# Attention order of a two-path decoder step: two steps of the item ahead between two scores of the next

## The chip, the cores and the metric

One core of a Trainium2 chip runs the whole program. The metric is the device time of one execution in microseconds, the median of three runs. PE is the matrix engine, DVE the vector engine, ACT the scalar engine, POOL the general engine, SP the queue that issues most DMAs.

## The reference, cut to what matters

The program is one inference step of a small decoder: a convolution layer, then keys and values from a single projection, then one layer of sparse attention, each followed by a gated feed-forward network, for a prompt of 512 rows and eight sample sequences of 8 rows. The changed part is the attention layer. It adds three softmax branches, each weighted by a sigmoid gate:

```
s_c = q . kc * scale - slope * d_c ; o_c = softmax(s_c, d_c >= 0) . vc      # compressed keys
s_s = q . ks * scale - slope * d_s ; o_s = softmax(s_s, d_s >= 0) . vs      # selected blocks
s_w = q . kw * scale - slope * d_w ; o_w = softmax(s_w, window) . vw        # sliding window
o = g[0] * o_c + g[1] * o_s + g[2] * o_w                                    # then o @ w_o
```

With 512 rows every block is selected, so the prompt computes two dense causal branches and a compressed one of 31 keys.

## The kernel before, in words

The prompt's attention is cut into 16 items, one for each of 4 key heads and 4 blocks of 128 query rows. `PROMPTS` gives their order as (key head, row block i); an item with row block i has rows of L = 128(i+1) keys. Items 0 to 15 have i = 1, 3, 3, 1, 1, 2, 3, 0, 3, 0, 2, 0, 2, 1, 2, 0. Each item goes through these steps:

- `score` n.a, four times (L2173 on PE): q times keys for two heads of one branch into a pair of PSUM banks. DVE adds the slope term, writes the row to `Pp` and takes its minimum (L1615); ACT takes the exponential and the row's sum (L1075). There are two bank pairs, so a score on PE waits until DVE is through with the last but one.
- `cmp` n (L2184 on PE): the same for the compressed branch into `Pc`; DVE L1625 to L1632, then ACT L1116.
- `weigh` n: DVE turns sums into weights (L1641 to L1652), the last of these scaling `Pc`; POOL multiplies the eight rows of `Pp` by them (L676), the four of the first branch first.
- `turn` n.x (L1776 on PE): the transposes of one block of 128 keys for four heads. Block 0 is the compressed one and waits for the weights (L1652); block 1 is the first of the first branch and waits for POOL's first four multiplications. An item has 2(i+1)+1 blocks: 3, 5, 7 or 9. A copy to one of four buffers `PT` (DVE L1696 or ACT L1088, in turns) empties the bank; there are two such banks. A copy also waits until the product that read this `PT` buffer last is done.
- `prod` n.x (L2220 on PE): block times values, added up in PSUM.
- `out`: ACT rounds the sum to `Oh` (L1132), DVE writes the rest to `Ol` (L1741).

The samples have steps of their own: `s_keys`, `s_score`, `s_weigh`, `s_turn`, `s_prod` (L2290), `s_oturn`, with `SMP_FRONT` and `SMP_BACK` naming the group in which they stand.

`_attention_plan` writes all of these into one list, `ATT`. Each engine's program walks that list and emits its own part of each step, so the list is the order of PE, DVE, ACT and POOL alike, and an instruction that waits holds up all that stands behind it on its engine. A group j of the list holds the scores and `cmp` of item j (`new`), the turns and products of item j-1 (`old`, from `_back`), and the samples' steps. The first part of a group, `seq`, alternates scores with old steps; what is left of `old` is mixed with the samples' steps in `rest`, and `weigh` j is put in at place 4 of `rest`, or at its end if `rest` is shorter.

After the list comes the output projection with `w_o`. Its first weights go to the same memory as buffers of the samples (`PTs`), so SP loads them only after the last `s_prod`.

Of the kernel before, what the change touches and what calls it, by code (L numbers as in the profile page):

```python
# [136 lines left out]
def _blocks(n):  # L137

    i = KVI(n)[1]
    return [(2, 0)] + [(br, kb) for br in range(2) for kb in range(i + 1)]  # L140


def _back(n):

    steps = len(_blocks(n))
    out = []
    for x_ in range(0, steps, 2):
        out += [("turn", n, y) for y in range(x_, min(x_ + 2, steps))]
        if x_:
            out += [("prod", n, x_ - 2), ("prod", n, x_ - 1)]  # L150
    return out + [("prod", n, steps - 1)]


def _attention_plan():

    plan, items = [], []

    def put(m):
        plan.append(m)
        if m[0] == "s_prod" or m[0] == "prod" and m[2] == len(_blocks(m[1])) - 1:  # L160
            items.append(("sample" if m[0] == "s_prod" else "prompt", m[1]))
            plan.append(("out", len(items) - 1, 0))

    for j in range(len(PROMPTS) + 1):
        more = j < len(PROMPTS)
        new = [("score", j, a) for a in range(4)] + [("cmp", j, 0)] if more else []
        old = _back(j - 1) if j else [("s_gates", 0, 0), ("p_gates", 0, 0)] + [("vc", h, 0) for h in range(4)]
        seq = new[:1]
        for k in range(1, len(new)):
            seq += old[:1] + new[k:k + 1]  # L170
            old = old[1:]
        smp = []
        for b in range(NB):
            if SMP_BACK[b] == j:
                smp += [("s_turn", b, 0), ("s_turn", b, 1), ("s_prod", b, 0), ("s_oturn", b, 0)]
        for b in range(NB):
            if SMP_FRONT[b] == j:
                smp += [("s_keys", b, 0), ("s_keys", b, 1), ("s_score", b, 0), ("s_weigh", b, 0)]
        rest, n_old, n_smp = [], 0, 0
        while n_old < len(old) or n_smp < len(smp):  # L180
            if n_smp < len(smp) and (n_smp * max(len(old), 1) < n_old * len(smp) or n_old == len(old)):
                rest.append(smp[n_smp])
                n_smp += 1
            else:
                rest.append(old[n_old])
                n_old += 1
        if more:
            rest.insert(4, ("weigh", j, 0))
        for m in seq + rest:
            put(m)  # L190
    return plan, items


ATT, ITEMS = _attention_plan()
SLOT = {m: k for k, m in enumerate(m for m in ATT if m[0] in ("score", "cmp", "s_score"))}
TURN = {m: k for k, m in enumerate(m for m in ATT if m[0] in
# [2238 lines left out]
```

## Time and profile before

| | |
|---|---|
| median of 3 runs | 1767.98 us (1763.5 to 1768.83) |
| profiled execution: its own time, its span | 1751.85 us, 1750.1 us |
| busy share of the span | PE 93%, DVE 49%, ACT 36%, POOL 9% |
| mean granted clock of PE | 0.973 |
| attention, from the first score to the last product | 989 to 1235 us of the span |

The page gives busy time over the whole span. Outside the attention PE is busy nearly without a break; within it all four engines take turns, and the stretch has to be read for itself. Times in the rows below are microseconds from the start of the span, unless a column is marked otherwise.

### The profile page before, as it was taken

How to read it: one execution, taken by the hardware profiler on the slowest of the kernel's cores; microseconds unless marked ns; L12 is line 12 of the kernel's file. 1: busy time of each engine (PE TensorE's matmuls, PEld its weight loads, DVE VectorE, ACT ScalarE, POOL GpSimd, SP SyncE). 2: the span in 40 equal slices, each digit the busy share in tenths (PEclk: the TensorE clock that was granted, in tenths of full speed). 3: DMA queues.
4: the chain of work that ended last, by engine and by line, in shares of the span. 5: the costliest groups of instructions: out<-in, count | busy, mean ns of one | idle time of the engine just before them, and what ended most of it. 6: DMA issues, size and time to landing. Idle time of an engine off the chain costs nothing.

```text
span 1750.1 us, 33973 instructions
## 1 busy us (share of the span) xinstructions
PE 1620.8 (93%) x14265; PEld 1480.4 (85%) x14265; DVE 857.3 (49%) x1646; ACT 631.7 (36%) x1263; POOL 164.5 (9%) x284
## 2 busy tenths in 40 slices
PE   5899868999999999999999999889899999999996
PEld 4788747899999999999899755445789999999995
DVE  5899955563232223355344377666474233223234
ACT  4455566342221222232214556545243221122223
POOL 2000001300000000001100255333000000000000
PEclk8999989999999999998999999988999999999998
DMA  9999853633332333322313510110322232222311
GB/s 325 294 320 325 296 176 118 186 96 113 101 106 73 97 97 108 98 61 79 95 50 90 147 28 2 49 38 12 103 67 85 85 107 75 73 78 81 112 34 55
DMA packets 236401, 198.34 MB, mean 113 GB/s; under 512 B 7058, under 2 KB 195810, under 8 KB 235984
## 3 DMA queue, kind: packets, MB, share of 16 engines
q1 hardware_dynamic: 229600, 172.25, 32.4%
q0 software_dynamic: 6352, 23.88, 4.7%
q8 instruction: 113, 1.85, 0.4%
q14 instruction: 32, 0.26, 0.0%
q10 hardware_dynamic: 304, 0.10, 0.0%
HBM read 188.87 MB, written 11.20 MB: 114 GB/s over the span
## 4 chain that ended last, share of the span: by engine, by line
PE 78%; DVE 7%; DMA 7%; ACT 4%; issue 3%; POOL 1%; POOLq 0%; SPq 0%; DVEq 0%; ACTq 0%
PE ps L1796 58%; DMA ada<-in_w_ada_dram 4%; PE ps L1776 4%; PE ps L1847 4%; PE ps L1812 2%; PE ps L2173 2%; PE ps L2220 2%; PE ps L2098 1%; DMA xrows<-in_x_sample_dram 1%; PE ps L1834 1%; PE ps L2290 1%; DVE t L1230 1%; DMA C<-in_cache_kv_dram 1%; DVE wl L1164 1%; PE ps L2074 1%
## 5 line engine op out<-in xcount | busy, mean ns | idle before, releaser
L714 ACT ACTIVATE wh<-raw 128x1024 fp32r<-128x1024 f32 (+1 forms) x173 | 193.1, 1117 | 706.5 <-PE ps L1796 686.4
L1796 PE MATMUL ps<-Hh,wh 128*128 128x288 f32 x1952 | 425.1, 300 | 7.8 <-DVE Hl L1395 3.7
L1796 PE MATMUL ps<-Hh,wl 128*128 128x288 f32 x1952 | 420.4, 297 | 0.0
L1796 PE MATMUL ps<-Hl,wh 128*128 128x288 f32 x1952 | 420.3, 297 | 0.0
L1164 DVE TENSOR_TENSOR wl<-raw,wh 128x1024 fp32r<-128x1024 f32 (+1 forms) x173 | 223.7, 1293 | 225.3 <-ACT wh L714 224.4
L1796 PEld LDWEIGHTS ps<-Hh,wh 128*128 128x128 f32 x1952 | 317.2, 191 | 10.3 <-issue 7.4
L1796 PEld LDWEIGHTS ps<-Hh,wl 128*128 128x128 f32 x1952 | 316.2, 190 | 0.2
L1796 PEld LDWEIGHTS ps<-Hl,wh 128*128 128x128 f32 x1952 | 316.0, 189 | 0.2
L1796 PE MATMUL ps<-al,wh 128*128 128x288 f32 x616 | 132.0, 296 | 0.0
L1796 PE MATMUL ps<-ah,wh 128*128 128x288 f32 x616 | 131.9, 296 | 0.0
L1796 PE MATMUL ps<-ah,wl 128*128 128x288 f32 x616 | 131.9, 296 | 0.0
L1518 DVE TENSOR_TENSOR t<-ps,t 128x576 f32<-128x576 f32 x44 | 33.4, 758 | 169.0 <-PE ps L1796 167.3
L1320 DVE TENSOR_TENSOR rtmp<-ps,mods 128x64 f32<-128x64 f32 x40 | 9.0, 224 | 196.4 <-PE ps L1796 176.1
L1812 PE MATMUL ps<-ada,cpad 128*32 128x128 f32 x2048 | 71.3, 287 | 31.5 <-DMA ada<-in_w_ada_dram 27.1
L676 POOL TENSOR_TENSOR Pp<-Pp,wgt 128x256 f32<-128x256 f32 (+3 forms) x128 | 88.3, 722 | 118.3 <-DVE wgt L1646 118.3
L1796 PEld LDWEIGHTS ps<-ah,wl 128*128 128x128 f32 x616 | 99.3, 189 | 0.0
L1796 PEld LDWEIGHTS ps<-ah,wh 128*128 128x128 f32 x616 | 99.3, 189 | 0.0
L1796 PEld LDWEIGHTS ps<-al,wh 128*128 128x128 f32 x616 | 99.3, 189 | 0.0
L1812 PEld LDWEIGHTS ps<-ada,cpad 128*32 128x32 f32 x2048 | 56.8, 115 | 42.0 <-DMA ada<-in_w_ada_dram 32.4
L1075 ACT ACTIVATE Pp<-Pp,nmin 128x256 f32<-128x256 f32 (+3 forms) x128 | 70.3, 550 | 26.4 <-DVE nmin L1615 26.1
L1459 DVE SCALAR_TENSOR_TENSOR y<-u_p,wdT,y 128x512 f32<-128x512 f32 x98 | 73.1, 746 | 0.0
L1459 DVE SCALAR_TENSOR_TENSOR r<-u_p,wdT,r 128x512 f32<-128x512 f32 x98 | 73.1, 746 | 0.0
(336 smaller groups left out, 2261.8 us busy)
## 6 DMA issues: line engine op xcount, KB each, us to landing
ada<-in_w_ada_dram SPq DMA_DIRECT2D x64, 1024.0 KB, 8.3
raw<-in_ffn_w_up_dram SPq DMA_DIRECT2D x88, 512.0 KB, 3.8
raw<-in_ffn_w_down_dram SPq DMA_DIRECT2D x32, 704.0 KB, 4.6
raw<-in_conv_w_pw_dram SPq DMA_DIRECT2D x24, 512.0 KB, 9.0
raw<-in_w_kv_dram SPq DMA_DIRECT2D x12, 512.0 KB, 3.8
C<-in_cache_kv_dram POOLq DMA_DIRECT2D x32, 128.0 KB, 3.6
out_win_sample_dram<-in_state_win_dram POOLq DMA_DIRECT2D x8, 512.0 KB, 3.7
raw<-in_nsa_w_in_dram SPq DMA_DIRECT2D x8, 512.0 KB, 3.9
```

What stands on the lines that cost most here:

```text
L676: nc.gpsimd.tensor_tensor(Pp[:, n % 2, s, 0:L], Pp[:, n % 2, s, 0:L], wgt[:, n % 2, s:s + 1].to_broadcast([P, L]), ALU.mult).then_inc(S("s ...
L714: A(wh[:, u % RING, 0:K, 0:w], raw[:, u % RING, 0:K, 0:w], ACT.Copy).then_inc(hi_ready, 1)
L1075: A(Pp[:, n % 2, s, 0:L], Pp[:, n % 2, s, 0:L], ACT.Exp, scale=-1.0, bias=nmin[:, n % 2, s:s + 1], accum_out=sums[:, n % 2, s:s + 1]).then ...
L1164: V.tensor_tensor(wl[:, u % RING, 0:K, 0:w], raw[:, u % RING, 0:K, 0:w], wh[:, u % RING, 0:K, 0:w].bitcast(F32), ALU.subtract).then_inc(lo ...
L1459: V.scalar_tensor_tensor(acc[k % 2], u_p[:, j, bass.ds(i * per + k, TP)], wdT[:, bass.ds(i * (per * DC) + (k * DC + j), 1)], acc[k % 2], A ...
L1518: V.tensor_tensor(t, tile(u0 + 2 * p + 1), t, ALU.mult).then_inc(tile_free, 2)
L1776: return nc.tensor.transpose(out, in_, ident[0:in_.shape[0], 0:in_.shape[0]])
L1796: last = M(ps[0:w, 2 * s + h, 0:HT], wt[:, s, k, 0:w], rt[:, k, h * HT:(h + 1) * HT], start=(k == 0 and i == 0), stop=(k == K - 1 and i == 2))
L1812: last = M(strip_bank(s_)[32 * g:32 * g + 32], cpad[:, 4 * hf + k, :], ada[:, n % RING_ADA, k, g * P:g * P + P], start=(hf == 0 and k == 0 ...
L1847: last = M(ps[:, 2 * s + h, 0:HT], wt[:, s, k, :], rt[:, k, h * HT:(h + 1) * HT], start=(k == 0 and i == 0), stop=(k == K - 1 and i == 2))
L2173: last = M(ps[:, 2 * (k % 2) + par, 0:L], qT[rows_, 2 * kv + a // 2, P * i:P * i + P], keys[rows_, 2 * br + kv // 2, 0:L], start=True, sto ...
L2220: last = M(ps[64 * par:64 * par + 64, 6 + it % 2, 0:2 * P], v, PT[TURN[("turn", n, x_)] % 4][0:K].rearrange("p (g q) -> p g q", g=G)[:, pa ...
```

## The change

Between two scores of the next item stand two steps of the item ahead, where there was one. Nothing else is edited; the steps, their number and their instructions are the same.

```
         seq = new[:1]
         for k in range(1, len(new)):
-            seq += old[:1] + new[k:k + 1]
-            old = old[1:]
+            seq += old[:2] + new[k:k + 1]
+            old = old[2:]
```

`seq` takes eight old steps in place of four, so `rest` is shorter by four. An item of five blocks has ten old steps, one of three blocks has six; for these `rest` may be shorter than four, and `weigh` goes to its end, behind `out`.

On PE, at the end of group 4 and the start of group 5 (both old items have five blocks). Before, from the compressed scores of item 4: five products and one turn of item 3, then a score of item 5 (L2173, 384 wide), the turn of item 4's block 0 (`Pc`), and a second score; behind it stands the turn of block 1 (`Pp`).

```order
L2184 MATMUL ps<-kcT_p_68,qT_65 128x31 x4
L2220 MATMUL ps<-PT2_99,vc_p_69 64x256 x2
L2220 MATMUL ps<-PT3_100,vrow_81 64x256 x2
L1776 MATMUL ps<-ident_124,Pp_101 128x128 x4
L2220 MATMUL ps<-PT0_97,vrow_81 64x256 x2
L2220 MATMUL ps<-PT1_98,vrow_81 64x256 x2
L2220 MATMUL ps<-PT2_99,vrow_81 64x256 x2
L2173 MATMUL ps<-kvT_64,qT_65 128x384
L2173 MATMUL ps<-Ksw_82,qT_65 128x384
L1776 MATMUL ps<-ident_124,Pc_102 31x128 x4
L2173 MATMUL ps<-kvT_64,qT_65 128x384
L2173 MATMUL ps<-Ksw_82,qT_65 128x384
```

The same place on PE in the changed kernel:

```order
L2184 MATMUL ps<-kcT_p_68,qT_65 128x31 x4
L2220 MATMUL ps<-PT1_98,vrow_81 64x256 x2
L2220 MATMUL ps<-PT2_99,vrow_81 64x256 x2
L2173 MATMUL ps<-kvT_64,qT_65 128x384
L2173 MATMUL ps<-Ksw_82,qT_65 128x384
L1776 MATMUL ps<-ident_124,Pc_102 31x128 x4
L1776 MATMUL ps<-ident_124,Pp_101 128x128 x4
```

Between `cmp` and the turn of block 1 stood five products, a turn, two scores and the turn of block 0; now two products, one score and the turn of block 0 stand there.

On DVE at the same place, before: the compressed scores, a copy, the weights of item 4, and then `Ol` of item 3.

```order
L1632 TENSOR_TENSOR Pc_102<-Pc_102,slk_144 128x124
L1696 COPY PT2_99<-ps 128x512
L1641 TENSOR_REDUCE sums_92<-Pc_102 128x4
L1643 RECIPROCAL wgt_93<-sums_92 128x12
L1646 TENSOR_TENSOR wgt_93<-wgt_93,gates_89 128x8
L1647 TENSOR_TENSOR wgt_93<-wgt_93,gates_89 128x4
L1652 TENSOR_TENSOR Pc_102<-Pc_102,wgt_93 128x124
L1741 TENSOR_TENSOR Ol_67<-ps,Oh_66 128x2x128
```

And in the changed kernel:

```order
L1632 TENSOR_TENSOR Pc_102<-Pc_102,slk_144 128x124
L1741 TENSOR_TENSOR Ol_67<-ps,Oh_66 128x2x128
L1641 TENSOR_REDUCE sums_92<-Pc_102 128x4
L1643 RECIPROCAL wgt_93<-sums_92 128x12
L1646 TENSOR_TENSOR wgt_93<-wgt_93,gates_89 128x8
L1647 TENSOR_TENSOR wgt_93<-wgt_93,gates_89 128x4
L1652 TENSOR_TENSOR Pc_102<-Pc_102,wgt_93 128x124
```

`Ol` moved ahead of the weights, and the copy is no longer between.

On DVE in group 8 (old item of three blocks) of the changed kernel, the last two scores of item 8 with `Ol` of item 7 between them; before, the copy of a turn stood there and `Ol` came behind the weights of item 8.

```order
L1615 ISA Pp_101,nmin_91<-ps,dist_115 128x512
L1615 ISA nmin_91 128x1
L1741 TENSOR_TENSOR Ol_67<-ps,Oh_66 128x2x128
L1615 ISA Pp_101,nmin_91<-ps,dist_115 128x512
L1615 ISA nmin_91 128x1
L1615 ISA Pp_101,nmin_91<-ps,dist_115 128x512
L1615 ISA nmin_91 128x1
L1625 TENSOR_TENSOR Pc_102<-ps,distc_137 128x2x31 x2
```

All three products of item 7 and its `out` are now done within the scores of item 8.

## Rows read from the trace of the kernel before

**Rows 1.** Windows: busy us (instructions) of each engine, granted clock, DMA share, GB/s.
```profile
988.00:1240.00 252.00, 220.55 (x2125) 126.75 (x2124) 173.04 (x607) 137.99 (x431) 100.52 (x146) 0.95 0.18 49
...
1150.60:1160.80 10.20, 9.77 (x46) 6.51 (x47) 6.22 (x31) 5.27 (x20) 2.22 (x6) 0.50 0.01 2
1177.90:1191.50 13.60, 11.52 (x124) 6.89 (x124) 4.21 (x17) 3.14 (x12) 5.82 (x9) 0.50 0.30 79
```

**Rows 2.** Waits within 988 to 1240: us in total, times, longest.
```profile
PEld ps L1776 <- ACT PT L1088: 7.9, 13, 1.0
```

**Rows 3.** Pieces of the chain that ended last: start, us, what.
```profile
995.46 0.59 PE ps L2184 x8
...
1001.86 1.06 PE ps L2173 x4
...
1008.92 4.08 POOL Pp L676 x4
...
1041.48 1.46 PE ps L2290 x56
1042.93 1.01 PE ps L2220 x8
...
1058.66 0.59 PE ps L1776 x4
1059.25 0.87 PE ps L2173 x4
...
1064.28 3.23 POOL Pp L676 x4
```

**Rows 4.** Timeline from `cmp` of item 4 to its turn of block 1; idle before in brackets.
```profile
1050.90 0.63 PE L2184 MATMUL ps<-kcT_p,qT 64*128 64x31 f32 x8
...
1051.58 0.35 DVE L1625 TENSOR_TENSOR Pc<-ps,distc 128x62 f32<-128x62 f32 x2 [0.34 <-PE ps L2184]
...
1052.99 0.31 ACT L1116 ACTIVATE Pc<-Pc 128x124 f32<-128x124 f32 x1 [0.35 <-DVE Pc L1632]
...
1053.92 0.27 DVE L1641 TENSOR_REDUCE sums<-Pc 128x4 f32<-128x124 f32 x1
...
1054.74 3.51 POOL L676 TENSOR_TENSOR Pp<-Pp,wgt 128x256 f32<-128x256 f32 x6 [11.90 <-DVE wgt L1646]
...
1054.77 0.38 ACT L1132 ACTIVATE Oh<-ps 128x256 fp32r<-128x256 f32 x1 [1.48 <-PE ps L2220]
...
1055.42 0.41 DVE L1741 TENSOR_TENSOR Ol<-ps,Oh 128x256 fp32r<-128x256 f32 x1
...
1057.16 0.66 PE L1776 MATMUL ps<-ident,Pp 128*128 128x128 f32 x4
```

**Rows 5.** Timeline of PE: turn of block 1 of item 1; score of item 11.
```profile
1013.05 0.66 PE L1776 MATMUL ps<-ident,Pp 128*128 128x128 f32 x4 [1.21 <-POOL Pp L676]
...
1151.03 0.58 PE L2173 MATMUL ps<-kvT,qT 64*128 64x128 f32 x1 [2.01 <-DVE nmin L1615]
```

**Rows 6.** Timeline of group 8: an exponential, `cmp`, and the first `s_prod`.
```profile
1104.72 0.71 ACT L1075 ACTIVATE Pp<-Pp,nmin 128x512 f32<-128x512 f32 x1
1104.83 0.64 PE L2184 MATMUL ps<-kcT_p,qT 64*128 64x31 f32 x8
...
1108.16 0.43 PE L2290 MATMUL ps<-Cs,PTs 128*32 128x64 f32 x16 [1.20 <-ACT PTs L1104]
```

**Rows 7.** Timeline of group 7, behind `s_score` of sample 2.
```profile
1094.55 0.69 DVE L1696 COPY PT<-ps 128x512 f32<-128x512 f32 x1 [3.19 <-PE ps L2220]
...
1095.16 0.48 DVE L1664 CUSTOM_DVE_ANT_0 Ps<-ps,tabs 128x320 f32<-128x320 f32 x1
...
1097.70 0.65 PE L2220 MATMUL ps<-PT,vrow 128*64 128x256 f32 x4 [1.24 <-ACT PT L1088]
```

**Rows 8.** Chain and timeline at the end of the attention.
```profile
1229.94 5.75 DMA raw<-in_nsa_w_o_dram
...
1239.86 0.82 PE L1796 MATMUL ps<-Oh,wh 128*128 128x288 f32 x2 [4.45 <-DVE wl L1164]
```

## Prediction

> **What bounds the kernel now.** The page puts most of the span on PE, so I read the attention alone, by windows. In its 252 us PE is busy for 220.55 [rows 1], which leaves 31.5 us of idle time: the whole of what a new order could win, as the order changes no instruction. The idle time is spread over many short waits. The view of waits shows who is waited for: PE's transposes wait 7.9 us, in 13 waits, for ACT's copies [rows 2], the largest share that has one cause. POOL waits for the weights, 11.90 us before item 4 [rows 4]: it has little to do, but it does it late, right before PE needs it. The chain of work then gives the price of each step on PE from its start to the next one's: a score is 1.06 us at 512 keys and 0.87 at 384, a turn 0.59, two products 1.01, `cmp` 0.59, `s_prod` 1.46 [rows 3]; for a score of 128 keys I estimate 0.42 from these. Last I read the timeline at every place where one item hands over to the next.
>
> The scores themselves hardly wait: score, turn, score, turn run at 1.06 + 0.59 and 0.87 + 0.59 in the chain, with PE as its only member. More cover between two scores is therefore worth nothing there. What counts is where the cover is taken from.
>
> **The hand-over of five-block items.** The chain from `cmp` of item n to its turn of block 1 is read from item 4 [rows 4]. `cmp` starts at 1050.90; DVE begins 0.68 later, and ACT's exponential starts at 1052.99 and lasts 0.31, so it ends 2.40 after `cmp`'s start. The weights start 0.82 before POOL does (1053.92 to 1054.74). POOL's first half ends and the turn starts 2.42 later (1057.16). With nothing in between this is 2.40 + 0.82 + 2.42 = 5.6 us for 256 keys. PE has to have that much work between the two steps, or it idles.
>
> Before, item 4 has five products (2.6), two turns (1.2), two scores (1.7) and `cmp` (0.6) there, 6.1 us for a distance of 6.26: an idle time of 0.2. After, it has `cmp`, two products, one score and one turn: 0.59 + 1.01 + 0.87 + 0.59 = 3.06 us. The chain has also grown, as `Ol` now stands ahead of the weights on DVE and needs `Oh`, which stands behind the exponential on ACT: 0.38 + 0.41 [rows 4] and two handovers, 0.85. So the turn of block 1 starts 6.5 us after `cmp`, PE idles 3.4, and the loss is 3.2.
>
> The same sum for the three others of this kind. Item 5 has 384 keys: POOL 3.23 [rows 3] in place of 2.42, distance 7.3, work 0.59 + 1.01 + 1.06 + 0.59 = 3.25, idle 4.05, against 0.35 before by the same count: 3.7. Item 1 has 512 keys: POOL 4.08 [rows 3], distance 8.2, idle 4.95, against 1.21 [rows 5] and 0.2 at the turn before it: 3.5. Item 0: no `out` is ahead, distance 5.6, work 0.59 + 1.06 + 0.59 = 2.24, idle 3.4 against 0.6: 2.8. **Together 13.2.** The bounds are 9 (the queue of DVE is emptier and the weights come 1 us earlier in each case, against my reading) and 16 (it is fuller: before, item 1 took 0.7 more than the bare chain).
>
> **Items behind three-block items (8, 10, 12).** Their group has `cmp`, then the samples' turns and `s_prod`, whose input is copied by DVE and ACT behind the compressed scores. Before, `s_prod` started 3.33 us after `cmp` with 1.20 of idle time [rows 6]. Two things change. The two products 7.0 and 7.1, 1.1 us, that stood around `cmp` are now ahead of the last score. And `Ol` stands between the last two scores on DVE: it waits for ACT to take the second exponential of the score before (0.71, [rows 6]), then 0.38 for `Oh` and 0.41 for itself, 1.5 us in which the last score isn't processed. Item 8 loses 2.6. For 384 keys I take 2.2 each. **Together 7.0**, bounds 1.8 (only one product's cover, 0.6 each) and 8.
>
> **Item 14.** Its `weigh` now has behind it only `s_prod`, a score of 128 keys and a turn, and ahead of it `Ol` of item 13. From `cmp`, work is 0.59 + 1.01 + two sample turns 0.95 + 1.46 + 0.15 + 0.42 + 0.59 = 5.2; the chain is 2.4, about 1.0 for copies of the sample's turns on DVE, 0.85 for `Oh` and `Ol`, 0.4 of handovers, 3.23 for POOL, 7.9. Idle 2.8 against 0.75 before: **2.1** (bounds 1 and 3). Items 2, 3, 6 to 13 have a sample's steps or many old steps behind `weigh` (6.8 us or more of work from `cmp`), so I cost them at nothing; item 6 is at the edge, with 1.0 of new idle time in exchange for as much that it had a few steps later.
>
> **The end.** The weights of `w_o` are fetched once the last `s_prod` is through: the DMA starts at 1229.94, takes 5.75, and PE idles 4.45 until 1239.86 [rows 8]. The change puts a turn and a product of item 14, that stood behind the last `s_prod`, ahead of it: 0.59 + 0.5, **1.1**, with nothing to hide it.
>
> **What is gained.** In groups 2, 7 and 9 a copy on DVE waits 3.19 us for a product that PE has behind `s_score` [rows 7], since both use one `PT` buffer. It holds up DVE's part of `s_score`, which starts at 1095.16, and the last product, which idles 1.24. In the new order that product stands ahead of `s_score`. DVE can then start when `s_score` ends, 1.25 earlier, but the two products no longer fill PE either: idle about 1.0, gain 0.3, three times. The waits for such copies at turns 5 and 6 and at `s_keys` in groups 2, 3, 7 and 9 come to about 4 of the 7.9 us [rows 2], of which I take 2.6 as gone. In groups 6, 11 and 13 the last product waited 0.4 to 0.5 and two turns 0.2 to 0.3 for the same reason: 2.0. **Together 5.5 less**, bounds 0 and 10; the upper one is the 7.9 us and the rest of the three gaps.
>
> **The clock.** In two stretches of the attention, 10.2 and 13.6 us long, the granted clock is 0.50, which is 1.2 GHz, in place of 1.00; the first began while PE idled for 2.01 us [rows 5]. PE is busy for 9.77 and 11.52 us in them [rows 1]. At full clock that work takes at least half of it, so one costs at most 4.9 and 5.8. The new order makes some seven gaps of 2.3 to 3.8 us. I take **6.0** more, a little over one such stretch, between minus 8 (both present ones gone) and plus 30.
>
> The Trainium skill (TensorE: Matmul & The Clock Gate, HAM oscillation) says that gaps in PE's work make the gate halve its rate, so that the work behind each gap starts slow. By that rule, applied to every gap, the clock would cost about 34 and not 6. This trace agrees only in part: the clock fell at the gap of 2.01 us, and at those of 1.20 to 1.24 it did not [rows 5 to 7].
>
> **The sum.** 13.2 + 7.0 + 2.1 + 1.1 - 5.5 + 6.0 = 23.9 us on an execution of 1751.85 (span 1750.1 and 1.75 around it): 1775.8, or 1.37% more. The three runs have their median at 1767.98, 0.9% above the profiled execution, so the forecast is 1767.98 x 1.0137 = 1792.
>
> **The rivals.** (A) *The clock falls at every new gap.* Seven times 4.9 is 34 in place of 6: 1751.85 + 17.9 + 34 = 1804, by the median 1820. For it speaks that the gaps are longer than the one ahead of 1150; against it, that several of them are broken by a turn, and pieces of 1.2 us kept the full clock [rows 5 to 7]. (B) *Faster: the copies stop blocking, and POOL's half is covered.* If the weights come as early against PE's work as they do now, only the gain remains, 5.5 to 10, and the time is 1758 to 1762. It decides at the turn of block 1: it wins if the distance from `cmp` is no longer than PE's work of 3.1 to 3.3 us. The bare chain of 5.6 speaks against that, since POOL alone takes 2.4 to 4.1 of it. (C) *No change.* The idle time at the hand-overs lets DVE and ACT catch up and is won back in the next scores. That needs scores that wait for DVE or ACT, and the chain shows PE alone there. 1768. (D) *Half of it:* the three-block items lose only one product's cover and the clock stays as it is: 13.2 + 1.8 + 2.1 + 1.1 - 5.5 = 12.7, by the median 1781, at the lower side of the forecast.
>
> **How the numbers follow.** The forecast's own case, with (D) in it, has 0.76, A 0.13, B 0.05, C 0.06. The range reaches from 1777, a little under (D), to 1806, which takes in a clock loss of 20; it leaves out most of A, and B and C. A measurement of this kernel tells 0.3% from no change, 5 us. Faster 0.05, same 0.05, slower 0.90 (a part of C is a small loss).
>
> **What would show it.** In the trace after: the turn of block 1 of items 0, 1, 4 and 5 waits for POOL with 1 to 3 us of idle time, and the turn of block 0 ahead of it for DVE's L1652 with 2 to 3; `s_prod` in groups 8, 10 and 12 waits about 3.5 us; DVE's L1741 in group 8 waits for ACT; the last product of groups 2, 7 and 9 waits 1.0; `w_o`'s DMA starts as many us later as the attention has lost. PE's busy time in the attention stays at 220, but for the clock. The prediction is wrong if the DVE part of `cmp` starts much earlier or later than 0.7 us behind PE's, or if the clock drops more often.

## Result: 2.6% slower, in the attention alone, and about half of it by the clock

| | before | changed |
|---|---|---|
| median of the runs | 1765.74 us (4 runs, 1760.65 to 1768.83) | 1806.76 us (4 runs, 1799.87 to 1810.04) |
| ratio of the two | | 1.0257, interval 1.0214 to 1.0299 |
| profiled execution, its time and span | 1751.85, 1750.1 us | 1799.87, 1798.1 us |
| mean granted clock of PE | 0.973 | 0.952 |

The forecast was 1792 us, 1.37% more, with a range to 1806; the time lies above it. The direction was right and the size was about half.

The page after: busy time of each engine, and the granted clock in 40 slices, in tenths.

```profile
PE 1645.6 (92%) x14265; PEld 1494.9 (83%) x14265; DVE 860.0 (48%) x1649; ACT 634.0 (35%) x1260; POOL 164.7 (9%) x284
...
PEclk8999989999999999999999898877799999999997
```

The instructions of PE are as many as before, yet PE is busy for 1645.6 us and not 1620.8. The digits of the clock say why: in slices 23 to 29, the attention, they read 8 9 8 8 7 7 7. The windows after, of the attention and of three stretches in it (columns as in [rows 1]):

```profile
985.00:1288.00 303.00, 246.97 (x2126) 143.02 (x2125) 175.83 (x610) 140.05 (x428) 100.59 (x146) 0.83 0.15 41
...
1209.20:1222.80 13.60, 10.64 (x134) 6.77 (x128) 4.89 (x18) 2.37 (x9) 6.36 (x8) 0.50 0.30 79
1134.10:1144.30 10.20, 8.79 (x85) 6.06 (x86) 5.13 (x21) 2.73 (x12) 8.07 (x8) 0.50 0.58 155
1168.20:1178.50 10.30, 8.59 (x114) 6.05 (x115) 3.59 (x14) 2.50 (x9) 6.35 (x8) 0.50 0.33 103
```

Against [rows 1] the attention is 51 us longer (303 for 252). PE is busy 26.4 us longer (246.97 for 220.55) and idle 24.6 us longer (56.0 for 31.45). The mean clock is 0.83 in place of 0.95. With two levels, 1.00 and 0.50, that is about 103 us at 1.2 GHz (303 x 0.17 / 0.5) against 25. So there are two halves to explain: waits, and work at the lower clock. What lies behind the attention is as long as before, and what lies ahead of it 3 us shorter. The profiled execution before took 14 us less than its median and the one after 7 less, so the traces show a loss of 48 us where the medians show 41.

The waits after, in 985 to 1288 (us, times, longest). The first row answers to POOL's wait in [rows 4], the others are PE's own; before, the most that PE's transposes waited for one engine was [rows 2]. A `PEld` row and a `PE` row of the same line are mostly the same waits, seen at the weight load and at the matmul.

```profile
POOL Pp L676 <- DVE wgt L1646: 180.0, 16, 15.8
...
PEld ps L1776 <- DVE Pc L1652: 11.7, 4, 3.3
...
PE ps L1776 <- ACT PT L1088: 9.4, 6, 2.9
...
PE ps L2290 <- ACT PTs L1104: 9.0, 4, 3.2
...
PE ps L1776 <- DVE Pc L1652: 8.6, 4, 2.5
...
PEld ps L1776 <- POOL Pp L676: 8.3, 6, 2.4
```

The first transposes of an item now wait four times for the weights (L1652) and six for POOL, `s_prod` waits for the samples' copies, and transposes wait 9.4 us for ACT's copies on PE, where it was 3.4 before.

**The hand-over of item 4**, timeline after. It answers to [rows 4].

```profile
1060.33 0.64 PE L2184 MATMUL ps<-kcT_p,qT 64*128 64x31 f32 x8
...
1061.01 0.35 DVE L1625 TENSOR_TENSOR Pc<-ps,distc 128x62 f32<-128x62 f32 x2 [0.35 <-PE ps L2184]
...
1062.42 0.31 ACT L1116 ACTIVATE Pc<-Pc 128x124 f32<-128x124 f32 x1 [1.58 <-DVE Pc L1632]
1062.64 0.37 ACT L1132 ACTIVATE Oh<-ps 128x256 fp32r<-128x256 f32 x1
1063.04 0.42 DVE L1741 TENSOR_TENSOR Ol<-ps,Oh 128x256 fp32r<-128x256 f32 x1 [0.65 <-ACT Oh L1132]
1063.38 0.27 DVE L1641 TENSOR_REDUCE sums<-Pc 128x4 f32<-128x124 f32 x1
...
1064.19 3.52 POOL L676 TENSOR_TENSOR Pp<-Pp,wgt 128x256 f32<-128x256 f32 x6 [12.03 <-DVE wgt L1646]
...
1065.00 0.62 PE L1776 MATMUL ps<-ident,Pc 128*31 128x128 f32 x4 [2.18 <-DVE Pc L1652]
...
1066.62 1.12 PE L1776 MATMUL ps<-ident,Pp 128*128 128x128 f32 x4 [0.99 <-POOL Pp L676]
```

From `cmp` to the turn of block 1 it is 6.29 us here and was 6.26 before: the chain of DVE, ACT and POOL has hardly changed, its cover on PE has. PE idles 2.18 and 0.99 us on the way.

**The third turn**, timeline after, of item 11 at the start of group 12. It is a wait that the forecast didn't have.

```profile
1196.14 0.18 DVE L1679 RECIPROCAL wgtS<-sumsS 128x3 f32<-128x3 f32 x1 [1.05 <-ACT Pcs L1126]
...
1196.56 0.79 DVE L1684 TENSOR_SCALAR Pcs<-Pcs,wgtS 128x15 f32<-128x15 f32 x1
...
1197.26 0.41 DVE L1741 TENSOR_TENSOR Ol<-ps,Oh 128x256 fp32r<-128x256 f32 x1
1197.60 0.54 DVE L1615 CUSTOM_DVE_ANT_0 Pp<-ps,dist 128x384 f32<-128x384 f32 x1
...
1199.39 0.57 ACT L1088 ACTIVATE PT<-ps 31x512 f32<-31x512 f32 x1
...
1200.11 0.63 PE L1776 MATMUL ps<-ident,Pp 128*128 128x128 f32 x4 [2.59 <-ACT PT L1088]
```

Read from below: PE waits 2.59 us for ACT to empty the bank of the item's first turn. ACT does that behind the exponentials of the score. The score's part on DVE starts only at 1197.60, though PE gave the score at 1194.77, because DVE stands in the weights of a sample (L1679), which wait for ACT. The same wait is 2.87 us at item 6, 1.95 at 10, 1.91 at 12 and 2.61 at 13; at items 10 and 12 it is for the copy on DVE. There is a second change at this place: between an item's first turn and its third, which needs the same bank, stood two scores and a turn, and now one score and a turn.

**`s_prod` of group 8**, timeline after. It answers to [rows 6].

```profile
1127.89 0.53 PE L2184 MATMUL ps<-kcT_p,qT 64*128 64x31 f32 x8
...
1128.59 0.43 DVE L1741 TENSOR_TENSOR Ol<-ps,Oh 128x256 fp32r<-128x256 f32 x1 [1.25 <-ACT Oh L1132]
...
1131.44 0.41 DVE L1712 COPY PTs<-ps 128x256 f32<-128x256 f32 x1
...
1132.54 0.43 PE L2290 MATMUL ps<-Cs,PTs 128*32 128x64 f32 x16 [3.21 <-ACT PTs L1104]
```

`Ol` waits 1.25 us for `Oh` with the last score behind it, and `s_prod` 3.21 us in place of 1.20.

**The end**, chain and timeline after, which answer to [rows 8]; and the last product of item 6, which answers to the last of [rows 7].

```profile
1278.29 6.68 DMA raw<-in_nsa_w_o_dram
```

```profile
1287.57 0.82 PE L1796 MATMUL ps<-Oh,wh 128*128 128x288 f32 x2 [5.30 <-DVE wl L1164]
...
1119.80 0.44 PE L2220 MATMUL ps<-PT,vrow 128*64 128x256 f32 x2 [1.15 <-ACT PT L1088]
```

### The profile page after: what moved, and what is told of

The parts are those of the page before. It is cut to its first block, busy times and chain, and to the rows that moved or that the text cites. A ratio compares the mean times of both kernels' runs of the same rounds, so it can differ in the third digit from the quotient of the medians.

```text
span 1798.1 us, 33973 instructions
## 1 busy us (share of the span) xinstructions
PE 1645.6 (92%) x14265; PEld 1494.9 (83%) x14265; DVE 860.0 (48%) x1649; ACT 634.0 (35%) x1260; POOL 164.7 (9%) x284
## 3 DMA queue, kind: packets, MB, share of 16 engines
q8 instruction: 113, 1.85, 0.4%
## 4 chain that ended last, share of the span: by engine, by line
PE 78%; DVE 7%; DMA 6%; ACT 4%; issue 3%; POOL 1%; POOLq 0%; SPq 0%; DVEq 0%; ACTq 0%
PE ps L1796 56%; PE ps L1776 5%; PE ps L1847 4%; DMA ada<-in_w_ada_dram 4%; PE ps L1812 2%; PE ps L2220 2%; PE ps L2173 2%; PE ps L2098 1%; DMA xrows<-in_x_sample_dram 1%; POOL Pp L676 1%; PE ps L1834 1%; PE ps L2290 1%; DVE t L1230 1%; DVE wl L1164 1%; DMA C<-in_cache_kv_dram 1%
## 5 line engine op out<-in xcount | busy, mean ns | idle before, releaser
L1776 PEld LDWEIGHTS ps<-ident,Pp 128*128 128x128 f32 x320 | 44.1, 169 | 41.5 <-issue 19.0
L1776 PE MATMUL ps<-ident,Pp 128*128 128x128 f32 x320 | 59.8, 331 | 19.9 <-ACT PT L1088 8.8
```

Source lines behind the costliest of these rows:

```text
L1776: return nc.tensor.transpose(out, in_, ident[0:in_.shape[0], 0:in_.shape[0]])
```

## Experiments

The ratio of each is to the kernel before, run beside it on the same chip.

### The clock: work in the gaps

The changed kernel, with fillers ahead of the steps that wait longest (three of the 17 entries of the table are shown; the bank is that of the next product):

```
+FILL = {('turn', 0, 0): 9, ('turn', 1, 0): 10, ('turn', 1, 1): 8, ...}
...
             for m in ATT:
                 what, n, x_ = m
+                if m in FILL:
+                    it_ = ORD[("prompt" if what == "turn" else "sample", n)]
+                    if it_ >= 2:
+                        pe.wait_ge(S("o_free"), it_ - 1)
+                    for _f in range(FILL[m]):
+                        M(ps[:, 6 + it_ % 2, 0:P], ident[:], ident[:], start=True, stop=True)
```

> The changed kernel with filler matmuls on PE (128x128 of ones and zeros into the PSUM bank of the next product, whose content is overwritten) put ahead of 17 steps that wait 0.8 to 3.2 us in its trace; 3 to 13 of about 0.2 us each, some four fifths of each gap. Theory 1, the clock: over half of the 45 us lost is work at 1.2 GHz behind the gaps (in the profiled run 99 us of the attention at that clock against 24 before, PE busy 27 us longer, PE idle only 24 us longer). With the gaps filled the time at 1.2 GHz falls under 50 us and the whole time by 12 to 25 us against the changed kernel, to 1.3% above before or less. Rival, the waits alone: the hand-overs cost 45 us through DVE, ACT and POOL and the clock is only seen beside them. Then fillers change nothing or add up to 10 us.

Measured: 1778.62 us, ratio 1.0092 (1.0062 to 1.0122). Its windows over the attention, and its timeline at the hand-over of item 4, with the fillers at L2313:

```profile
993.00:1267.00 274.00, 247.31 (x2418) 158.07 (x2416) 176.05 (x610) 139.48 (x428) 100.50 (x146) 0.98 0.17 45
```

```profile
1068.73 2.27 PE L2313 MATMUL ps<-ident 128*128 128x128 f32 x18
1070.98 0.62 PE L1779 MATMUL ps<-ident,Pc 128*31 128x128 f32 x4
1071.44 1.06 PE L2313 MATMUL ps<-ident 128*128 128x128 f32 x8
1072.59 0.66 PE L1779 MATMUL ps<-ident,Pp 128*128 128x128 f32 x4
```

The turns start as late as without fillers, since they wait for the same things: from `cmp` to the turn of block 1 it is 5.98, 8.08, 6.29 and 7.14 us for items 0, 1, 4 and 5 in both traces. But the clock is 0.98 in place of 0.83, and the attention is 29 us shorter. Work that computes nothing takes 1.65 of the 2.57%, some 29 us, a little more than I expected. Theory 1 holds; the rival falls. (The kernel before loses time to the clock too, so these 29 us aren't all a cost of the change; the kernels with fillers below tell how much is.)

The same with transposes as fillers:

```
-                    for _f in range(FILL[m]):
-                        M(ps[:, 6 + it_ % 2, 0:P], ident[:], ident[:], start=True, stop=True)
+                    for _f in range(FILL[m] * 3 // 2):
+                        tr(ps[:, 6 + it_ % 2, 0:P], ident[:])
```

> The changed kernel with the same fillers as the first of these runs, but as transposes in place of matmuls, half as many more of them, as one takes about 0.15 us and not 0.2. With matmuls the time was 0.9% over before and the clock stayed at 2.4 GHz for all but 7 us. If any work on PE holds the clock up, it is the same here, within 5 us. If transposes don't count, the clock falls as in the changed kernel and the time is 2% or more over before.

Measured: 1782.88 us, ratio 1.0126 (1.0073 to 1.0178), and in the attention:

```profile
988.00:1264.00 276.00, 243.98 (x2341) 152.02 (x2341) 175.37 (x610) 139.55 (x428) 100.62 (x146) 0.95 0.17 45
```

A clock of 0.95 against 0.83 without fillers and 0.98 with matmuls, or 24 us at 1.2 GHz against 99 and 7, in one execution each; the two intervals of the time overlap. Transposes hold the clock up here, if perhaps a little less well.

The next two are the kernel before with fillers, first at 11 places, 3 to 8 each, and 18 ahead of the output projection (the same helper, called with the product's number by hand):

```
+FILL = {('s_prod', 1, 0): (8, 4), ('score', 11, 2): (14, 8), ('s_turn', 5, 1): (17, 6), ('prod', 1, 8): (2, 4), ...}
```

> The kernel before with the same fillers, 3 to 8 of them ahead of 11 steps that wait 0.8 to 2.0 us there, and 18 in the gap ahead of the output projection. If the clock costs what the fillers on the changed kernel say (29 us of the attention for 92 us less at 1.2 GHz), the 24 us at that clock here are worth some 7 us: 4 to 8 us faster than before. If fillers only helped because they lay in long gaps, or if they cost as much as they bring, within 3 us of before.

Measured: 1751.13 us, ratio 0.9969 (0.9947 to 0.9991). With fillers at three more places:

> The kernel before with fillers at three more places (before turns 1.5 and 6.2 and s_score of sample 7, 2 to 6 each). The last 10 us at 1.2 GHz in the attention should go too, worth 3 us: 0.3 to 0.6% faster than before. If the fillers now stand in PE's way, it is no faster than the version with 11 places.

Measured: 1751.10 us, ratio 0.9949 (0.9921 to 0.9977). Windows of both over the attention, the one with 11 places first:

```profile
989.00:1239.00 250.00, 231.96 (x2260) 139.93 (x2258) 172.75 (x607) 137.87 (x431) 100.67 (x146) 0.98 0.18 50
```

```profile
989.00:1240.00 251.00, 233.65 (x2283) 142.47 (x2282) 172.78 (x607) 138.09 (x431) 100.68 (x146) 0.99 0.18 49
```

Both are faster than the kernel before, and the second is the fastest version here; whether it beats the first can't be told. By the ratios they bring 5.5 and 9 us, as expected. The attention in the traces is only 1 to 2 us shorter, but the profiled execution before had a mean clock of 0.973, where its runs beside these experiments have 0.955 to 0.974.

These two tell the clock's part in the change. With matmuls as fillers both kernels are at 2.4 GHz in the attention for all but 7 to 10 us, and the changed one is still 1.2 to 1.4% slower (1.0092 against 0.9969 and 0.9949), or 22 to 25 us, of which 1 to 2 us are the fillers ahead of the output projection that it doesn't have. That is the part of the waits; it fits the 24.6 us that PE is idle longer. The other 20 to 25 of the 45 us are the clock.

### Which items carry the loss

Two steps behind items of seven or nine blocks only, and in the other kernel behind those of three or five only:

```
-            seq += old[:2] + new[k:k + 1]
-            old = old[2:]
+            two = 2 if len(_blocks(max(j - 1, 0))) >= 7 and j else 1
+            seq += old[:two] + new[k:k + 1]
+            old = old[two:]
```

> Two steps between scores only where the item ahead has seven or nine blocks; one step, as before, behind items of three or five. By my sum the loss sits at the short items: 13.2 us at four hand-overs, 7.0 behind three-block items, 2.1 at item 14, and two of the new waits at the third turn (items 11 and 13, 5 us) as well, while the long items gain 3 to 5. So PE's idle time returns to that of before or 4 less, the clock falls about as before or for 20 us more, and the time is within 8 us of before on either side. Rival, that two steps are bad for every item (banks of the turns fill up): it keeps at least half of the loss, 20 us or more.

> The complement: two steps only behind items of three or five blocks. If the loss sits at the short items, PE idles 25 us more than before and the clock adds 15 to 25: 35 to 50 us slower than before, all or more of the loss of the whole change. Rival as for the other half: 20 us or less.

Measured: 1772.69 us, ratio 1.0061 (1.0038 to 1.0085), and 1791.83 us, ratio 1.0186 (1.0132 to 1.0240). The windows of the attention of the first and of the second:

```profile
990.00:1259.00 269.00, 230.09 (x2126) 133.17 (x2127) 174.77 (x609) 139.27 (x429) 100.48 (x146) 0.91 0.17 46
```

```profile
987.00:1277.00 290.00, 241.06 (x2129) 140.80 (x2128) 174.25 (x608) 139.55 (x430) 100.66 (x146) 0.86 0.15 43
```

The two parts add up to 2.47%, nearly the whole 2.57%. Three quarters are with the short items, as the forecast had it, though it is a little less than I expected of that half (1.9% for 2.0 to 2.8). But the long ones gain nothing; they lose 0.6%, 11 us, where I had expected 8 at most on either side. The trace of that kernel shows where: the third turns of items 6, 10 and 12 wait 2.87, 3.09 and 1.97 us.

A smaller dose, one step everywhere but behind the nine-block items, and there 1, 2, 2 and 2:

```
+            two = (1, 2, 2, 2)[k - 1] if j and len(_blocks(j - 1)) in (9,) else 1
```

> One step between the scores as before, except behind the four items of nine blocks, where it is 1, 2, 2, 2. That keeps the cover of the second turn and of the hand-overs and should leave the gain at the copies: 0.3 at the last product and most of the waits at turns 5 and 6 and at s_keys, 3 us in all. 1 to 5 us faster than before. Rival: the gain isn't there because the copies wait for something else; within 1 us, or slower.

Measured: 1763.12 us, ratio 1.0029 (1.0003 to 1.0054): not faster. Its last product of item 6 waits 1.67 us, where [rows 7] have 1.24:

```profile
1099.38 0.44 PE L2221 MATMUL ps<-PT,vrow 128*64 128x256 f32 x2 [1.67 <-ACT PT L1089]
```

### The order between the scores, or the rest of the group

```
-            seq += old[:2] + new[k:k + 1]
-            old = old[2:]
+            two = (1, 2, 2, 3)[k - 1]
+            seq += old[:two] + new[k:k + 1]
+            old = old[two:]
```

> The changed kernel with 1, 2, 2 and 3 old steps between the scores in place of four times 2: the rest of each group is the same, only the second turn stands one score later. The waits at the third turn of items 6, 10, 11, 12 and 13 (2 to 2.9 us each, 12 in all) should fall to what the kernel before had at the score there, 2 us in one place, since the bank of the first turn has one more score to come free; and each hand-over to items 0, 1, 4, 5 has one score more cover (0.6 to 1.06 us). So PE idles 8 to 13 us less than in the changed kernel, and with the clock the time falls by 12 to 25 us. Rival: the waits come from the rest of the group being short, whatever stands between the scores: less than 5 us.

Measured: 1808.30 us, ratio 1.0270 (1.0217 to 1.0323). The third turn of item 6:

```profile
1107.36 0.66 PE L1777 MATMUL ps<-ident,Pp 128*128 128x128 f32 x4 [3.21 <-ACT PT L1089]
```

It waits 3.21 us (2.87 in the changed kernel), and the others 1.81, 2.44, 1.31 and 2.46. That doesn't test the banks, though: with 1, 2, 2 and 3 the second turn and a score change places, and between the first turn and the third stand one turn and one score as in the changed kernel, where the kernel before has two scores. My expectation of one score more was wrong. The next kernel leaves the scores alone and puts `s_score` two steps of PE earlier in groups 6, 11 and 13; with it `s_keys` and `s_weigh` stand one step earlier, so that the end of these groups is that of the kernel before:

```
+        if j in (6, 11, 13):
+            rest = [smp[0], old[0], smp[1], old[1], smp[2], old[2], old[3], smp[3]] + old[4:]
```

> The changed kernel with the samples' s_score of groups 6, 11 and 13 two steps of PE earlier, so that behind it stand a turn and three products, as in the kernel before, in place of two products. Theory: the third turn of items 6, 11 and 13 waits (2.6 to 2.9 us in the changed kernel) because DVE and ACT are still busy with s_score's reductions and exponentials when the next group starts. Then these three waits fall by about 1.1 us each, the two steps' time, and those of items 10 and 12, which have s_score last in their group in both kernels, stay at 2. Rival: the wait belongs to the order between the scores; it stays in all five within 0.3 us.

Measured: 1799.60 us, ratio 1.0221 (1.0168 to 1.0274). The third turn of item 6:

```profile
1105.16 0.55 PE L1778 MATMUL ps<-ident,Pp 128*128 128x128 f32 x3 [1.19 <-ACT PT L1090]
```

2.87 became 1.19, item 11's 2.59 became 0.91, item 13's 2.61 became 0.88; item 10, with `s_score` and `s_weigh` last in its group in all kernels, stays at 1.98, and item 12 goes from 1.91 to 1.49. So 1.7 us of the wait at each of items 6, 11 and 13 comes from `s_score` and `s_weigh`, moved together here, standing too near the end of a group that the change has made shorter. The time alone, 0.4% less with overlapping intervals, wouldn't show it.

The rest comes from the order between the scores, and the kernels that change some groups only separate the two. Idle time of PE between the first turn and the third of an item, in us, from their traces:

| | 6 | 10 | 11 | 12 | 13 |
|---|---|---|---|---|---|
| before | 0.88 | 2.27 | 0.04 | 0.54 | 0.00 |
| changed | 3.18 | 1.95 | 2.59 | 1.91 | 2.61 |
| the order around the third turn changed, the group ahead as before | 1.37 | 3.09 | 1.03 | 1.97 | 0.93 |
| the group ahead changed, the order as before | | 1.40 | 1.54 | 1.30 | 1.54 |

"The group ahead" is the one in which the item's own scores stand. In the third line item 6 is from the kernel with 1, 2, 2 and 2, items 10 and 12 from that with the long items alone, and 11 and 13 from that with the short ones alone; the fourth line has the short ones at 10 and 12 and the long ones at 11 and 13. Three of these turns, in the order 6, 10, 11:

```profile
1084.61 0.66 PE L1777 MATMUL ps<-ident,Pp 128*128 128x128 f32 x4 [1.37 <-ACT PT L1089]
...
1163.12 0.55 PE L1777 MATMUL ps<-ident,Pp 128*128 128x128 f32 x3 [3.09 <-DVE PT L1697]
...
1196.47 0.63 PE L1777 MATMUL ps<-ident,Pp 128*128 128x128 f32 x4 [1.03 <-ACT PT L1089]
```

At items 11 and 13 the two changes add up: 1.0 for the score that no longer stands between the two turns, 1.5 for the shorter group. At item 10 the wait isn't new; it stood at a score before [rows 5] and has moved to the turn.

### Ol and out

`weigh` of items 1, 4, 5 and 14 at the head of the rest, ahead of `out`:

```
-            rest.insert(4, ("weigh", j, 0))
+            rest.insert(0 if j in (1, 4, 5, 14) else 4, ("weigh", j, 0))
```

> The changed kernel with weigh of items 1, 4, 5 and 14 put at the head of the rest of its group, ahead of out, in place of behind it. If Ol ahead of the weights on DVE is 0.85 us of each of these waits, PE idles 3 us less, and with the clock behind it the time falls by 3 to 8 us against the changed kernel. If the lost cover on PE is all that matters and the weights were not held up, nothing changes (under 2 us).

Measured: 1806.32 us, ratio 1.0261 (1.0210 to 1.0312), no gain. In its trace the first turns of items 1, 4 and 5 wait 0.6 us less each (1.88, 1.57 and 1.19 for 2.48, 2.18 and 1.78). Item 1 gives 0.3 of it back at the next turn, and in group 14 `s_prod` of sample 6 now waits 2.34 us for copies that stand behind the weights. `Ol` ahead of the weights is a real but small part of the wait.

`out` of items 7, 9 and 11 put behind `cmp`:

```
+    for q, j in ((7, 8), (9, 10), (11, 12)):
+        o_ = ("out", items.index(("prompt", q)), 0)
+        plan.remove(o_)
+        plan.insert(plan.index(("cmp", j, 0)) + 1, o_)
```

> The changed kernel with the out of the three-block items 7, 9 and 11 put behind cmp of the next item, in place of ahead of its last score. My sum says that of the 2.0 us that s_prod waits longer than before in groups 8, 10 and 12, Ol between the scores on DVE is 1.5 and the lost cover 1.1. Then s_prod waits 1.0 to 1.5 us less in each of the three and the time falls by 3 to 8 us, clock included. If the cover alone counts, the waits stay within 0.3 us.

Measured: 1804.19 us, ratio 1.0253 (1.0208 to 1.0299). DVE and `s_prod` in group 8:

```profile
1141.51 0.42 DVE L1745 TENSOR_TENSOR Ol<-ps,Oh 128x256 fp32r<-128x256 f32 x1 [0.64 <-ACT Oh L1136]
...
1142.60 0.43 PE L2294 MATMUL ps<-Cs,PTs 128*32 128x64 f32 x16 [3.11 <-DVE PTs L1719]
```

3.11 us for 3.21. That doesn't clear `Ol`: it now waits behind the compressed scores and holds up the samples' copies instead. So the next kernel keeps two products, and with them `out`, back until after `cmp`:

```
-            seq += old[:2] + new[k:k + 1]
-            old = old[2:]
+            two = 2 if j not in (8, 10, 12) else (2, 2, 0, 0)[k - 1]
+            seq += old[:two] + new[k:k + 1]
+            old = old[two:]
```

> The changed kernel with 2, 2, 0 and 0 old steps between the scores of items 8, 10 and 12, which leaves two products of the three-block items behind cmp, as before. The waits of s_prod in groups 8, 10 and 12 are 3.2, 2.8 and 2.7 us in the changed kernel and 1.2, 1.3 and 0.8 before; putting Ol behind cmp left them as they were. If it is the products' cover, each falls by 1.0 to 1.5 us. If the last score comes too late on DVE for some other reason, it stays.

Measured: 1808.96 us, ratio 1.0262 (1.0208 to 1.0315). `s_prod` of group 8:

```profile
1139.08 0.43 PE L2291 MATMUL ps<-Cs,PTs 128*32 128x64 f32 x16 [1.34 <-ACT PTs L1105]
```

1.34, 1.07 and 1.07 us in the three groups, for 3.21, 2.80 and 2.69: the wait is undone. Cover and `Ol` went together here, so no run separates them. The distances do: from `cmp` to `s_prod` it was 3.33 us before, 4.65 in the changed kernel, 4.55 with `out` late and 3.47 with both undone, so of the 2.0 us that `s_prod` waits longer 1.3 is delay on DVE and ACT; the other 0.7 is one product of cover. PE is idle less in this kernel, and yet the time is no better: some 5 us less of waiting, at three places, doesn't bring the clock back (106 us at 1.2 GHz in the trace, 99 in the changed kernel).

## Why the forecast was half right

**The hand-overs** (13.2 us). Right. The distances from `cmp` to the turn of block 1 came out at 5.98, 8.08, 6.29 and 7.14 us for items 0, 1, 4 and 5, against 5.6, 8.2, 6.5 and 7.3. The idle time of items 1, 4 and 5 is 4.43, 3.17 and 3.41, against 4.95, 3.4 and 4.05; with what was there before taken off, about 11 in all four. The distances before were 5.81, 7.97, 6.26 and 6.94, so against the kernel before it has grown by 0.03 to 0.2 and not by the 0.85 that I had added to the bare chain. `Ol` ahead of the weights is 0.6 of it, by the run with `weigh` first.

**Items behind three-block items** (7.0). Right in mechanism, too large: 2.0, 1.5 and 1.85 us more at `s_prod`, 5.4 in all. I had counted two products of cover where one was between `cmp` and `s_prod`.

**Item 14** (2.1). Right in kind: 0.26, 0.99 and 0.84 us of new gaps at `s_prod`, `s_oturn` and the turn of block 1, and a gap of 0.58 at a later turn is gone, 1.5 in all.

**The end** (1.1). In the trace: the last `s_prod` stands behind one more turn and one more product, and from there to the output projection it is as long as before, 11.9 us; PE idles 5.30 at the end for 4.45.

**All others at nothing.** This step failed. "Items 2, 3, 6 to 13 have a sample's steps or many old steps behind `weigh` [...], so I cost them at nothing" looked at `weigh` alone, and "More cover between two scores is therefore worth nothing there" overlooked that the two scores between an item's first turn and its third were cover for the copy that empties the bank. The shorter end of the group strikes the samples' `s_score` and `s_weigh`, the new order takes one of the two scores away, and both come out at the third turn of items 6, 10, 11, 12 and 13: PE idles 12.2 us between first and third turn, and 3.7 at the same places before, 2.0 of them in [rows 5]. So a term of 8.5 us was put at nothing; the table above shows both causes, each by itself.

**The gain at the copies** (5.5). Right in kind, too large. The last products of groups 2, 7 and 9 wait 1.15 for 1.24, 0.3 in all, where I had 0.9. PE's idle time at all turns from the fourth on and all products of the items with seven and nine blocks falls from 8.1 to 4.3 us, a gain of 3.8; `s_keys` of sample 0 takes 0.7 of it back. The kernel with the change behind nine-block items alone isn't faster but 0.3% slower. With all these the waits come to 24.6 us against 17.9.

**The clock** (6.0). The term that was mis-sized most. It measured 26 us in PE's busy time between the two traces, and 20 to 25 by the kernels with and without fillers. I had worked out 34 for "the clock falls at every new gap", as a rival with a chance of 0.13, and set it aside since gaps of 1.2 us had kept the full clock [rows 5 to 7] and a turn breaks several of the new ones. Neither reason held. At the hand-over of item 4, where a turn stands between gaps of 2.18 and 0.99 us, the clock fell too:

```profile
1065.90:1072.50 6.60, 5.88 (x20) 3.29 (x20) 2.43 (x7) 3.13 (x10) 2.95 (x6) 0.50 0.01 2
```

And `s_prod` of group 8 with its gap of 1.20 us kept the full clock in the trace before [rows 6], but in the kernel with 1, 2, 2 and 2 the same step with the same gap was followed by 10 us at 1.2 GHz:

```profile
1109.84 0.43 PE L2291 MATMUL ps<-Cs,PTs 128*32 128x64 f32 x16 [1.20 <-ACT PTs L1105]
```

```profile
1112.00:1122.00 10.00, 8.93 (x86) 5.60 (x86) 4.42 (x19) 3.24 (x13) 8.06 (x8) 0.50 0.55 143
```

So one trace was too little to say which gaps are harmless, and the sign that I had named, that the clock drops more often, came true. The rival's 1820 us is no nearer (13 us over the 1807 measured; my 1792 is 15 under), and its count was off as well: seven falls at 4.9 us each, where the trace has ten more than before, at 2.6 each. The Trainium skill (TensorE: Matmul & The Clock Gate, HAM oscillation) says that work behind a gap starts slow; its example is a wait for a DMA. This trace agrees at all four hand-overs of five-block items, where the clock was 0.50 behind the gaps, but not at the third turn of item 11, where it stayed at 1.00 for 8 us behind a gap of 2.59.

What stays open: which pattern of gaps makes the clock fall. The new gaps are longer (14 over 1.5 us, for one before), and more stretches ran at 1.2 GHz (12 for 2), but no run separates the length of the gaps from their number. Among the kernels with two steps everywhere, those that differ by 4 us of idle time stand at nearly the same clock, and the one with two products put back (4.5 us less idle time) had more work at 1.2 GHz; the earlier `s_score` raised the mean clock of the four runs a little, from 0.949 to 0.954. The fillers raised it most.

## What to carry to other kernels

When the steps of one item are moved forward, ask what they covered where they were: here some 4 us of small waits were gained, and chains through DVE, ACT and POOL that ended behind the moved steps came out uncovered for 28 us, some of them a group later. Price a new gap on PE twice, once as idle time and once as the work behind it at 1.2 GHz; the second was about half of the loss. Where a gap can't be closed, throwaway work on PE in a PSUM bank whose content is overwritten held the clock here and made even the kernel before 0.3 to 0.5% faster.

## What the runs showed of the hardware

- No gap on PE in the attention of the changed kernel is longer than 3.21 us, 14 are over 1.5, and about 100 of 303 us ran at 1.2 GHz. With the long gaps filled, all but some 7 us ran at 2.4 GHz.
- Transposes kept the clock up nearly as well as matmuls: 0.95 and 0.98 in the attention, against 0.83 without either.
- The same gap of 1.20 us at the same step was followed by full clock in one kernel's trace and by 10 us at 1.2 GHz in another's.
